# The order of four products in a step: long, long, short, short against long, short, long, short

## The reference, cut to what matters

```python
hn = rmsnorm(h, norm_mix_w[i])
z, xbc, dt_raw, u, g_a, g_b = jnp.split(hn @ w_in[i], splits, axis=-1)
y_a = mamba2_mixer(z, xbc, dt_raw, ...)            # ends in y @ w_proj
y_b = s5_mixer(u, ...)                             # y @ w_glu, split, sigmoid
merged = jax.nn.sigmoid(g_a) * y_a + jax.nn.sigmoid(g_b) * y_b
h = h + merged @ w_out[i]
hn = rmsnorm(h, norm_ffn_w[i])
h = h + conv_glu_ffn(hn, w_up[i], conv_ffn_w[i], conv_ffn_b[i], w_down[i])
return rmsnorm(h, norm_final_w)
```

## Time and profile before

| | |
|---|---|
| median of 3 runs | 1798.61 us (1798.23 to 1798.70) |
| profiled execution | 1798.7 us, span 1796.6 us |
| granted TensorE clock, mean | 0.996 of full speed |
| TensorE busy | 1763.5 us, 98% |
| VectorE busy | 1381.1 us, 77% |
| ScalarE busy | 959.7 us, 53% |
| weight DMA | 313.42 MB, 52.0% of the 16 DMA engines |

### The profile page before, as it was taken

One profiled execution on the slowest core, in us unless ns is written; L12 is line 12 of the kernel. 1 busy time (PEld: TensorE's weight loads), 2 busy tenths in 40 slices (PEclk: granted clock), 3 DMA queues, 4 the chain that ended last, 5 costly groups with the idle time before them and its releaser, 6 DMA issues.

```text
span 1796.6 us, 30327 instructions
## 1 busy us (share of the span) xinstructions
PE 1763.5 (98%) x9998; PEld 1510.7 (84%) x9998; DVE 1381.1 (77%) x1953; ACT 959.7 (53%) x1216; POOL 146.5 (8%) x216
## 2 busy tenths in 40 slices
PE   7999999999999999999999999999999999999997
PEld 6788888888878888888888888888888888888886
DVE  6799999999988888655687678888888888654544
ACT  6555555556655656565565554444444444444443
POOL 7800000001001010000000100000000000000000
PEclk9999999999999999999999999999999999999998
DMA  6455444455455555455556555555555555555552
GB/s 240 170 171 172 153 165 162 148 173 180 158 173 178 192 190 178 166 186 190 187 187 232 188 178 187 189 190 192 187 187 188 189 189 191 194 190 191 187 189 105
DMA packets 91413, 326.23 MB, mean 182 GB/s; under 512 B 11344, under 2 KB 12368, under 8 KB 91232
## 3 DMA queue, kind: packets, MB, share of 16 engines
q1 hardware_dynamic: 86320, 313.42, 52.0%
q0 software_dynamic: 5040, 12.11, 2.4%
HBM read 323.35 MB, written 2.15 MB: 181 GB/s over the span
## 4 chain that ended last, share of the span: by engine, by line
PE 90%; DVE 5%; ACT 2%; issue 2%; DMA 1%; DVEq 0%; SPq 0%; ACTq 0%
PE psum L1327 57%; PE psum L1329 28%; PE psum L1365 2%; PE psum L1373 2%; DVE dec L1077 1%; ACT whi L407 1%; DVE wlo L768 1%; PE psum L1412 1%; DVE dec L1083 1%; PE psum L1413 0%; ACT dec L583 0%; DMA xin<-in_x 0%; DMA raw<-in_w_u 0%; DVE bc L962 0%; DVE nw L798 0%
## 5 line engine op out<-in xcount | busy, mean ns | idle before, releaser
L768 DVE TENSOR_TENSOR wlo<-raw,whi 128x1024 fp32r<-128x1024 f32 x588 | 719.3, 1228 | 352.8 <-ACT whi L407 351.2
L407 ACT ACTIVATE whi<-raw 128x1024 fp32r<-128x1024 f32 x588 | 620.4, 1058 | 536.2 <-PE psum L1329 526.9
L1327 PE MATMUL psum<-act,whi 128*128 128x512 f32 x1792 | 575.7, 403 | 2.3 <-DVE ub L774 2.3
L1327 PE MATMUL psum<-nw,whi 128*128 128x512 f32 x1552 | 488.7, 396 | 4.5 <-DVE wlo L768 4.3
L1329 PEld LDWEIGHTS psum<-act,wlo 128*128 128x128 f32 x1792 | 337.3, 188 | 79.9
L1329 PE MATMUL psum<-act,wlo 128*128 128x256 f32 x1792 | 352.9, 278 | 0.0
L1329 PEld LDWEIGHTS psum<-nw,wlo 128*128 128x128 f32 x1552 | 291.5, 188 | 68.2
L1329 PE MATMUL psum<-nw,wlo 128*128 128x256 f32 x1552 | 306.3, 278 | 0.0
L1327 PEld LDWEIGHTS psum<-act,whi 128*128 128x128 f32 x1792 | 275.5, 189 | 20.7 <-DVE wlo L768 10.1
L1327 PEld LDWEIGHTS psum<-nw,whi 128*128 128x128 f32 x1552 | 236.9, 189 | 6.7 <-issue 3.2
L1327 PE MATMUL psum<-ff,whi 128*128 128x512 f32 x704 | 221.1, 395 | 0.0
(11 more groups left out here) (180 smaller groups left out, 1450.5 us busy)
## 6 DMA issues: line engine op xcount, KB each, us to landing
raw<-in_w_up SPq DMA_DIRECT2D x176, 512.0 KB, 4.3
raw<-in_w_zx SPq DMA_DIRECT2D x96, 512.0 KB, 3.2
raw<-in_w_down SPq DMA_DIRECT2D x88, 512.0 KB, 4.2
raw<-in_w_gate SPq DMA_DIRECT2D x64, 512.0 KB, 3.3
raw<-in_w_proj SPq DMA_DIRECT2D x48, 512.0 KB, 3.3
raw<-in_w_bc SPq DMA_DIRECT2D x32, 512.0 KB, 3.2
raw<-in_w_glu SPq DMA_DIRECT2D x32, 512.0 KB, 3.2
raw<-in_w_out SPq DMA_DIRECT2D x32, 512.0 KB, 3.9
```

The lines of the kernel that those rows point to most:

```text
L407: fn(whi[:, s, :], raw[:, s, :], ACTF.Copy).then_inc(hi_ready, 1)
L768: V.tensor_tensor(wlo[:, s, :], raw[:, s, :], whi[:, s, :], ALU.subtract).then_inc(lo_ready, 1)
L1327: mm(psum[:, b + t, :], whi[:, s, cols(t)], x, start=first, stop=False)
```

## The change

The order of the products inside a `k` is changed. Before, the long products of both tiles come first and then the short ones of both tiles. After, each tile's long product is followed at once by its short one. In `dt`, with its one tile, the order stays as it is. Operands, waits, flags and the signal at the unit's end stay.

```diff
@@ -1319,14 +1319,10 @@
                     row = 4 * q + k
                     x = act[:, row + (KT if name == "down" and row >= KT else 0), :]
                     first, last = q == 0 and k == 0, q == quads - 1 and k == 3
-                    tiles = range(1 if name == "dt" else 2)
-
-                    def cols(t):
-                        return slice(k * L + t * P, k * L + t * P + P)
-                    for t in tiles:
-                        mm(psum[:, b + t, :], whi[:, s, cols(t)], x, start=first, stop=False)
-                    for t in tiles:
-                        ins = mm(psum[:, b + t, L:2 * L], wlo[:, s, cols(t)], x[:, 0:L], start=False, stop=last)
+                    for t in range(1 if name == "dt" else 2):
+                        cols = slice(k * L + t * P, k * L + t * P + P)
+                        mm(psum[:, b + t, :], whi[:, s, cols], x, start=first, stop=False)
+                        ins = mm(psum[:, b + t, L:2 * L], wlo[:, s, cols], x[:, 0:L], start=False, stop=last)
                 ins.then_inc(unit_used, 1)
```

## The result

The changed kernel took 1808.58 us (median of 7, 1802.26 to 1811.23) against 1798.33 us (median of 7, 1796.96 to 1799.99): ratio 1.0055, 95% interval 1.0039 to 1.0072. It is slower by 10 us, where 6 us less was forecast. Its times are not one heap: 1802.26, 1802.78 and 1802.85, then 1808.58, 1810.05, 1810.71 and 1811.23. The result lists 19 more executions of the changed kernel: of all 26, seven lie from 1802.26 to 1803.88 and nineteen from 1807.47 to 1812.08. The kernel before showed no such gap in any run.

A forecast was written before the change was run, and what follows sets the result against it. TensorE, busy 98% of the span, was taken as the bound, through the spacing of its products. 2208 steps x 2.8 ns = 6.2 us off 1798.7 us gave 1792.5 us; the range was 1789.5 to 1800 us.

The forecast's parts named there:

- The order itself: All phases take dt's long-short pair, 0.347 us for 0.3484: 2.8 ns saved per step (four products of one k).
- Columns: In each step of four products, the sum of 1536 columns stays the same; price 0.
- weight loads: In each step, two of four weight loads lie under a short product in either order; price 0.
- same bank: A short product right behind its long one in one bank does not stall; price 0, upper bound 762 us excluded.
- What is not given back: Where TensorE already waits, at the head and in gate turns, 128 steps save nothing; 2208 steps x 2.8 ns remain.
- half rival: Change of bank is what costs, and two of four changes stay: 1.4 ns a step saved, 1795.6 us; chance 0.15.
- no change: A product's slot depends only on its columns, so the order does nothing: 1798.7 us; chance 0.28.
- The slower one: Rival: long-short turns cost more and double to four a step; 1804 us, upper end 1815 us; chance 0.15.
- A slot that depends on its columns alone: A TensorE product's slot depends on its own columns and nothing beside it, so the time stays 1798.7 us.
- second rival: The no change case: slots depend only on columns, dt's shorter pair is local to its 4 us; 1798.7 us, chance 0.28.
- What would make the prediction wrong: That dt's pair of 0.347 us is not representative: a second tile, another bank or a different stretch.

The follow-up runs named there:

- e10: The kernel before the change, profiled once more without an edit; 1799.15 us, one run.
- e7: The changed kernel with the fp32 products of the norm's sum in up moved one unit later; 1810.52 us, ratio 1.0067 to the kernel before.
- e3: All eight long products of a unit issued first, then its eight short ones; 1801.75 us, ratio 1.0020 to the kernel before.
- e6: The changed kernel with the first unit of each group in the order before; 1805.64 us, ratio 1.0044 to the kernel before.
- e8: The kernel before up to the sum in up, then one step in its order, then the changed order to the end; 1795.49 us, ratio 0.9987.
- e9: As e8, but with two steps in the order before behind the sum in up; 1808.68 us, ratio 1.0036 to the kernel before.

## Why the prediction was wrong, step by step

*The order itself* is the step that failed. The prediction took 0.347 us a pair, from 11 pairs of dt, for a property of the order. It is the fast one of two rhythms; the slow one is 0.353 to 0.354, and the kernel before shows it in dt as well (e10). Forecast 0.694 us a step, measured 0.6925 to 0.6933 in some phases and 0.7067 in others. In the profile after, up and down alone lost 10.5 us, where 2.8 ns on their 1056 steps should have won 3.0. The bounds of 0.8 to 4.0 ns came from the rounding of the starts, which bounds the reading and not the next execution; that was the fault in the range.

*Columns, weight loads, same bank*: priced at 0. The counts are the same. That the bank does not make the difference is borne out by glu, which has both speeds with the same banks (e7). That loads cost nothing is not shown: the slow rhythm may well be in how load and product meet, and no run separated them.

*What is not given back* (128 steps, 0.4 us) was not tested by itself. VectorE and ScalarE did not become a bound in any order.

*The rivals.* The half rival and no change were not seen. The slower one had the right side and size (1804 to 1815 us) and the wrong mechanism: a price for each turn between long and short. e3, with a quarter of the turns of the kernel before, was 3 us slower than it, and the fast rhythm, with the most turns, is the fastest of all.

*A slot that depends on its columns alone*, the ground of the second rival, failed too: the same two products take 347 or 353 ns together at one granted clock of 1.00. The Trainium skill (TensorE: Matmul & The Clock Gate, Back-to-back issue gap) gives a gap by columns alone only for a product that stands alone, and says that in a stream the loads and the products set the spacing together. That loads have a part in the two rhythms no run here shows.

*What would make the prediction wrong* was named, that dt's pair is not representative, and so was the row to look at, down, which took 248.4 us and not 243.9. The doubt was not taken seriously enough: there were 11 pairs, from one place, behind one wait.

What stays open is what in TensorE holds the rhythm. Shown is that alternation has two lasting ones, that neither phase, data nor bank decides, and that the kind of the paired step ahead of it agrees with the rhythm in six of six lead-ins that were planned and in the 126 of e6. That one step more or less moves most executions from one heap to the other is shown too (e8 and e9). Whether the kind makes the rhythm, or both are signs of one state of the engine, is not. Not shown is the part of the engine in which it lives, nor what sets the kind at the start of a stretch from one execution to the next. The best kernel here, e8, was faster in ten of eleven runs, by 3.5 us at the medians, which is 0.2%, and 10 us slower in the eleventh. It does not beat the kernel before in any way that one should rely on.

## What to carry to other kernels

A loop in which the bound engine waits for nothing can still run at two speeds: read its period in every stretch and in two profiles, and look at the single times for heaps, before a difference of 1% is put down to an order of instructions. A short stretch that happens to have the new order already is one draw, so ask for a second profile of the unchanged kernel first. An order that shows one period only, as long, long, short, short does here, may be worth more than one that is faster half of the time.

## What the runs showed of the hardware

Alternating products of 512 and 256 fp32r columns lock into 0.347 or 0.353 us a pair and stay there for over 700 us, over two phases, through loops, with the clock at 1.00. In the runs of 8, products of one kind take 0.230 and 0.120 us a product. The slow rhythm is made of two pairs of 0.35 us and one of 0.36. A single pair of products swapped ahead of them moved most executions by 14 us (from 1795 to 1809), though not all. The fp32 products of the sum in up turned the fast rhythm into the slow one in three profiles, and small fp32 products between the groups did not shake the slow one off in 29 places.
